# Fourteen seven-product pairs in each FFN, with sums by transfer, on a one-core transformer kernel

## What is computed

```
y    = x * rsqrt(mean(x*x) + EPS) * g           # per token
gate, up = split(y @ w_gu)                      # 1024 -> 2 * 2816
x    = x + 0.5 * ((silu(gate) * up) @ w_down)   # 2816 -> 1024
```

## Time and profile before

| | |
|---|---|
| median of 3 runs | 2190.74 us (2190.73 to 2190.77) |
| the profiled execution's own time | 2190.57 us |
| its span, first to last instruction | 2188.8 us |
| granted TensorE clock, mean | 1.000 |
| busy: PE, weight loads, DVE, ACT, POOL | 99%, 82%, 71%, 47%, 7% |

### The profile page before, as it was taken

The page is one execution under the profiler, slowest core; times in us unless marked ns, Lnnn a source line. Parts: engine busy times, 40 slices in busy tenths (PEclk is TensorE's granted clock), DMA queues, the critical chain, the costliest instruction groups (busy, mean ns, idle before and its releaser), DMA issues.

```text
span 2188.8 us, 30114 instructions
## 1 busy us (share of the span) xinstructions
PE 2173.2 (99%) x12152; PEld 1798.2 (82%) x12152; DVE 1564.9 (71%) x2421; ACT 1022.7 (47%) x1592; POOL 145.4 (7%) x112
## 2 busy tenths in 40 slices
PE   9999999999999999999999999999999999999999
PEld 7889897777778898988898887777788898977777
DVE  6768586988657685776777577777667685865873
ACT  5424244667544242334333245777544242438672
POOL 3000003000130000030000012000120000030000
PEclk9999999999999999999999999999999999999999
DMA  6333234131124334242423232222123333332211
GB/s 197 116 116 116 96 103 134 40 97 59 60 79 170 122 116 133 83 130 77 154 78 120 93 116 94 75 75 94 50 74 128 109 118 102 97 111 77 77 59 39
DMA packets 209714, 217.86 MB, mean 100 GB/s; under 512 B 3664, under 2 KB 205520, under 8 KB 209576
## 3 DMA queue, kind: packets, MB, share of 16 engines
q1 hardware_dynamic: 207184, 206.06, 29.1%
q0 software_dynamic: 1152, 5.44, 0.8%
q10 hardware_dynamic: 1240, 4.43, 0.5%
HBM read 213.79 MB, written 6.32 MB: 101 GB/s over the span
## 4 chain that ended last, share of the span: by engine, by line
PE 91%; DVE 4%; ACT 3%; issue 1%; DMA 0%; POOL 0%; SPq 0%; DVEq 0%; ACTq 0%
PE ps L1911 90%; PE ps L1915 1%; DVE sb_wlo L1278 1%; ACT sb_whi L730 1%; DVE sb_gla_ek L1617 0%; DVE sb_gla_eq L1620 0%; DMA sb_xT<-xT 0%; ACT sb_xh L730 0%; DVE sb_xT L1406 0%; ACT sb_hyb_th L730 0%; DVE sb_gla_xb L1612 0%; DVE sb_gla_cf L1609 0%; DVE sb_gla_d L1597 0%; DVE sb_xl L1300 0%; ACT sb_lnb L730 0%
## 5 line engine op out<-in xcount | busy, mean ns | idle before, releaser
L1911 PE MATMUL ps<-sb_xh,sb_whi 128*128 128x512 f32 (+1 forms) x1952 | 724.8, 371 | 1.8 <-DVE sb_xl L1700 0.8
L1911 PE MATMUL ps<-sb_xl,sb_whi 128*128 128x512 f32 (+1 forms) x1952 | 707.8, 364 | 0.1
L1911 PE MATMUL ps<-sb_xh,sb_wlo 128*128 128x512 f32 (+1 forms) x1952 | 705.7, 364 | 0.0
L730 ACT ACTIVATE sb_whi<-sb_raw 128x1024 fp32r<-128x1024 f32 (+1 forms) x368 | 377.7, 1033 | 360.5 <-PE ps L1911 353.0
L1278 DVE TENSOR_TENSOR sb_wlo<-sb_raw,sb_whi 128x1024 fp32r<-128x1024 f32 (+1 forms) x288 | 372.0, 1294 | 125.3 <-ACT sb_whi L730 123.7
L1911 PEld LDWEIGHTS ps<-sb_xh,sb_whi 128*128 128x128 f32 x1952 | 368.5, 189 | 76.7 <-issue 18.1
L1911 PEld LDWEIGHTS ps<-sb_xl,sb_whi 128*128 128x128 f32 x1952 | 368.8, 189 | 60.1 <-issue 3.1
L1911 PEld LDWEIGHTS ps<-sb_xh,sb_wlo 128*128 128x128 f32 x1952 | 368.4, 189 | 59.3
L1911 PE MATMUL ps<-sb_ffn_ah,sb_whi 128*128 128x512 f32 x704 | 275.3, 391 | 0.0
L1911 PE MATMUL ps<-sb_ffn_ah,sb_wlo 128*128 128x512 f32 x704 | 274.1, 389 | 0.0
L1911 PE MATMUL ps<-sb_ffn_al,sb_whi 128*128 128x512 f32 x704 | 273.9, 389 | 0.0
(11 more groups left out here) (288 smaller groups left out, 2593.3 us busy)
## 6 DMA issues: line engine op xcount, KB each, us to landing
sb_raw<-ffn_w_gu SPq DMA_DIRECT2D x86, 1024.0 KB, 5.2
sb_raw<-ffn_w_down SPq DMA_DIRECT2D x32, 1024.0 KB, 5.2
sb_raw<-w_ada SPq DMA_DIRECT2D x12, 1024.0 KB, 5.7
sb_raw<-ffn_w_down SPq DMA_DIRECT2D x16, 768.0 KB, 4.8
sb_raw<-gla_w_in SPq DMA_DIRECT2D x12, 1024.0 KB, 5.3
sb_raw<-diff_w_in SPq DMA_DIRECT2D x12, 1024.0 KB, 5.1
sb_raw<-w_in SPq DMA_DIRECT2D x10, 1024.0 KB, 5.2
sb_raw<-gla_w_out SPq DMA_DIRECT2D x4, 1024.0 KB, 5.1
```

The lines of the kernel that those rows point to most:

```text
L730: return e.activation(out, in_, func, bias=bias, scale=scale)
L1911: return e.matmul(out, lhsT, rhs, start=start, stop=stop, skip_group_check=skip)
```

## The change

Four edits are made together. FAST has fourteen pairs of each FFN instead of ten: 5, 10, 13 and 18 are added. The multiplication of up by the norm's factor goes away; the factor is multiplied onto each down sum instead, into a scratch tile (`gb`), and a second VectorE instruction adds that onto x. One of the four adds of `weight_sums` becomes a transfer issued by POOL, which adds a block of gate's weights onto up's in the raw panel (`gate_onto_up`). The low part of an activation is no longer VectorE's for all pairs but the last of a part: ACT writes minus the high part into `al`, and a transfer of POOL's queue adds the activation onto it. The sums of x are built in a buffer of their own (`ffn_xs`), which lies where four tiles of `al` are kept later. Half of the order on ACT and VectorE is rewritten to fit, and low parts of the activations have two more semaphores (`f_low0`, `f_low1`).

```diff
-FAST = ((6, 8, 9, 11, 12, 14, 16, 17, 19, 20),) * 4
+FAST = ((5, 6, 8, 9, 10, 11, 12, 13, 14, 16, 17, 18, 19, 20),) * 4
...
+            with ExitStack() as early:
+                x_sum[f] = sb(f"ffn{f}_xs", [128, 8, 256], F32, early)
+            al += tiles_of(sb(f"ffn{f}_al4", [128, 4, S], F32R, mem))
...
         def tail_late(j):
-            return j >= 5 and j not in (7, 15, 21)
+            return j >= 4 and j not in (7, 15, 21)
...
                         act(ah[:, j - k0, :], ub[j % 2][:, :], ACT.Copy).then_inc(sem["f_ah"], 1)
+                        if by_dma(J):
+                            act(al[j - k0], ub[j % 2][:, :], ACT.Copy, scale=-1.0).then_inc(sem["f_neg"], 1)
...
-                e.tensor_tensor(sums[:, 0:4, :], c_, d_, ALU.add).then_inc(sem["s_add"], 1)
-                w.wait_ge(sem["s_add"], 4 * i + 1)
-                e.tensor_tensor(c_, c_, a_, ALU.add).then_inc(sem["s_add"], 1)
-                e.tensor_tensor(sums[:, 4:8, :], sums[:, 0:4, :], a_, ALU.add).then_inc(sem["s_add"], 1)
-                w.wait_ge(sem["s_add"], 4 * i + 3)
+                w.wait_ge(sem[f"s_pre{i % 2}"], 16 * (i // 2 + 1))
+                e.tensor_tensor(sums[:, 4:8, :], c_, d_, ALU.add).then_inc(sem["s_add"], 1)
+                w.wait_ge(sem["s_add"], 3 * i + 1)
+                e.tensor_tensor(sums[:, 0:4, :], sums[:, 4:8, :], a_, ALU.subtract).then_inc(sem["s_add"], 1)
                 e.tensor_tensor(sums[:, 8:12, :], sums[:, 4:8, :], b_, ALU.add).then_inc(sem["s_add"], 1)
...
-                    def plain_up(j, u):
-                        used(w, u + 1)
-                        e.tensor_tensor(ub[j % 2][:, :], psum[f_banks[f]["pair", j][1]][:, :], rb[:, :],
-                                        ALU.mult).then_inc(sem["f_u"], 1)
...
+                    def up_free(j):
+                        if j >= 2 and by_dma(22 * f + j - 2):
+                            w.wait_ge(sem[low_done[22 * f + j - 2][0]], low_done[22 * f + j - 2][1])
...
-                            e.tensor_tensor(v, v, g, ALU.mult).then_inc(sem["f_p"], 1)
+                            up_free(j)
+                            used(w, u + 1)
+                            e.tensor_tensor(v, psum[f_banks[f]["pair", j][1]][:, :], g, ALU.mult).then_inc(sem["f_p"], 1)
...
-                        e.scalar_tensor_tensor(out=x[:, m, :], in0=psum[f_banks[f]["down", (part, m)][0]][:, :],
-                                               scalar=0.5, in1=x[:, m, :], op0=ALU.mult,
-                                               op1=ALU.add).then_inc(sem["f_x"], 1)
+                        e.scalar_tensor_tensor(out=gb[m % 2], in0=psum[f_banks[f]["down", (part, m)][0]][:, :],
+                                               scalar=0.5, in1=rb[:, :], op0=ALU.mult,
+                                               op1=ALU.mult).then_inc(sem["f_t"], 1)
+                        w.wait_ge(sem["f_t"], part_x(f, part, m))
+                        e.tensor_tensor(x[:, m, :], x[:, m, :], gb[m % 2], ALU.add).then_inc(sem["f_x"], 1)
...
-                w.wait_ge(sem["f_join"], 4 * i + 4)
-                e.tensor_tensor(up, up, rb[:, :], ALU.mult).then_inc(sem["f_u"], 1)
...
+            def gate_onto_up(f, j):
+
+                if j in FAST[f]:
+                    i = fast_before[f] + FAST[f].index(j)
+                    gate, up, off = fast_panels[i]
+                    for q in (gate, up):
+                        w.wait_ge(sem[f"raw{q % NRAW}"], 16 * (q // NRAW + 1))
+                    if i >= 2:
+                        w.wait_ge(sem["s_add"], 3 * i - 3)
+                    e.dma_start(raw[up % NRAW][:, 0:4, off:off + 128], raw[gate % NRAW][:, 0:4, off:off + 128],
+                                accum_op=ALU.add).then_inc(sem[f"s_pre{i % 2}"], 16)
+
+            def low_parts(f):
+
+                _, al, _, ub, _, _, _, _ = ffn_mem[f]
+                for k0, n in FF_PARTS[f]:
+                    for j in range(k0, k0 + 4):
+                        gate_onto_up(f, j)
+                    for j in range(k0, k0 + n):
+                        if j + 4 < k0 + n:
+                            gate_onto_up(f, j + 4)
+                        if by_dma(22 * f + j):
+                            w.wait_ge(sem["f_neg"], neg_made[22 * f + j])
+                            e.dma_start(al[j - k0].bitcast(F32), ub[j % 2][:, :],
+                                        accum_op=ALU.add).then_inc(sem[low_done[22 * f + j][0]], 16)
```

More of the change, by code:

```diff
@@ L581, in fast_source @@
             return raw[panel % NRAW][:, 0:nk, off:off + 128]
+        fast_panels = [(*W.fast[u][:2], W.units[u][1]) for u in W.fast if W.units[u][3] == "fa"]
         def lo_done(w, u):
@@ L674, in build, with by_dma @@
         f_banks = [ffn_banks(f) for f in range(4)]
+        low_done, n_vec, n_dma = {}, 0, [0, 0]
+        for f in range(4):
+            for k0, n in FF_PARTS[f]:
+                for j in range(k0, k0 + n):
+                    if FAST[f] and j < k0 + n - 1:
+                        n_dma[j % 2] += 1
+                        low_done[22 * f + j] = f"f_low{j % 2}", 16 * n_dma[j % 2]
+                    else:
+                        n_vec += 1
+                        low_done[22 * f + j] = "f_al", n_vec
+        def by_dma(J):
+            return low_done[J][0] != "f_al"
+        neg_made = rank([J for J in range(88) if by_dma(J)])
         def h_evac(w, k):
@@ L773, in ffn @@
             def ffn(f):
-                ah, _, gb, ub, _, sums, th, _ = ffn_mem[f]
+                ah, al, gb, ub, _, sums, th, _ = ffn_mem[f]
                 u = first[f"ffn{f}"]
@@ L821, in ffn @@
                         if j < 4:
-                            scaled_x(f, j, sums)
+                            scaled_x(f, j, x_sum[f])
                         silu(j)
@@ L833, in ffn @@
                             e.dma_start(bias_vec, bias_rows[:, :]).then_inc(sem["bias_dma"], 16)
[L834 to L840, removed]
                         if j < 4:
                             w.wait_ge(sem["t_vec"], 4 * (t_before[f] + j) + 3)
-                            act(th[:, j, :, :], sums[:, 8:16, :], ACT.Copy).then_inc(sem["t_act"], 1)
+                            act(th[:, j, :, :], x_sum[f][:, 4:8, :], ACT.Copy).then_inc(sem["t_act"], 1)
+                    if f == 2 and part == 0:
+                        w.wait_ge(sem["d_lam_mm"], 1)
+                        act(lam[:, 2:4], psum[FFN_AUX][:, 0:2], ACT.Exp).then_inc(sem["d_lam_e"], 1)
                     last = part == len(parts) - 1
@@ L1359, in ffn @@
                         if after_fast:
-                            scale_halves(f, j - 1, vgw[(j - 1) % 2], ub[(j - 1) % 2][:, :])
-                            product(j - 1)
+                            product(j - 1, None)
                         w_lo(u + 1)
@@ L1376, in ffn @@
                         u += 2
+                        if j < 4:
+                            x_sums(f, j, x_sum[f])
                         if not tail_late(j):
-                            plain_up(j, u - 2)
-                        if j < 4:
-                            x_sums(f, j, sums)
-                        if not tail_late(j):
-                            product(j)
+                            product(j, u - 2)
                         if j < 4:
                             w.wait_ge(sem["t_act"], t_act_before[f] + 3 * j + 3)
-                            e.tensor_tensor(tl[:, j, :, :], sums[:, 8:16, :],
+                            e.tensor_tensor(tl[:, j, :, :], x_sum[f][:, 4:8, :],
                                             th[:, j, :, :].bitcast(F32), ALU.subtract).then_inc(sem["t_vec"], 1)
@@ L1922, in rows @@
                     k = k0 + t
-                    w.wait_ge(sem[ready[0]], ready[1] + k + 1 + (h_y_ready[k] if ready[0] == "h_ylo" else 0))
+                    if ready[0] == "f_al":
+                        w.wait_ge(sem["f_ah"], ready[1] + k + 1)
+                        w.wait_ge(sem[low_done[ready[1] + k][0]], low_done[ready[1] + k][1])
+                    else:
+                        w.wait_ge(sem[ready[0]], ready[1] + k + 1 + (h_y_ready[k] if ready[0] == "h_ylo" else 0))
                     mm(psum[bank][:, :], hi[:, t, :], H[k], start and t == t0, False)
@@ L2013, in ffn @@
                             u += 1
-                        emptied[b] = "f_x", part_x(f, part, m)
+                        emptied[b] = "f_t", part_x(f, part, m)
                         if (part, m) in ADA_SUM:
@@ L2542, in pool_program @@
                 sum_squares(m)
+            low_parts(0)
             ffn_squares(0, KT)
```

79 lines of the change are left out of this document (39 added, 40 removed).

## The result

The changed kernel takes 2210.27 us (median of 4 runs, 2209.09 to 2211.32) against 2190.73 for the kernel before: ratio 1.0089, 95% interval 1.0073 to 1.0105. It is slower by 19.5 us. My 2192.0 and the range up to 2202 were both too low. The profiled execution after has a span of 2209.4 us, 20.6 more than before.

The account below looks back on a forecast made before the run. TensorE, busy 99% of the span, was taken to bound the kernel. 2190.57 - 12.8 for matmuls + 14.1 for new waits gave 2191.9, set at 2192.0 us against the median; range 2178 to 2202.

Parts of the forecast that it names:

- Matmuls: TensorE, all FFNs: 16 more fast pairs save 0.80 us each, 12.8 us in all.
- VectorE in runs: Consecutive fast pairs 8 to 14: VectorE needs 9.4 us per pair, below TensorE's 10.08, so no wait.
- The tail: Last-part down sums: 0.72 us more per step, making waits of 3.7, 4.7, 5.0 and 0.7 us at FFN ends.
- the last term: End of FFN 3 to the last block: one addition, 0.72 less 0.1, a wait of 0.7 us.
- The clock: TensorE after the new waits at FFN ends: forecast with no fall to 1.2 GHz, so no cost.
- rival A: New FFN-end waits drop TensorE's clock, 2.5 us a fall, three give 2199.5; chance 0.27.
- Transfers: POOL's queue in fast pairs: 256 KB transfers take 3.7 us and cost nothing; they cost only above 6.7 each.
- Rival C: Late transfers hold the third join of fast pairs; from 6.7 us each they delay TensorE, 2204 at 7.0; chance 0.15.
- Rival B: FFN ends: the added waits are hidden in full or by two thirds, giving 2177.9 to 2187; chance 0.20.
- the 14.1 us: Sum of the forecast new TensorE waits at the ends of the four FFNs.
- The likeliest case: Whole kernel: the forecast with the ends of its per-pair and tail-step terms, 2189.5 to 2194.5 us.

Follow-up runs that it names:

- e8: e3 with pair 5 plain again in FFN 1 alone: 2178.15 us.
- e10: e9 with the low parts of all activations made by VectorE again, without their transfers and second ScalarE copies: 2177.99 us.
- e12: e10 with the fourth weight sum on VectorE too, leaving POOL's queue no transfer in the FFNs: 2187.10 us.
- e5: The kernel before, with each down sum in the last part of each FFN made by two VectorE instructions: 2213.88 us.
- e3: The changed kernel with the norm's factor multiplied onto up again in each FFN's last part, one VectorE instruction per down sum there: 2188.98 us.
- e6: e3 with the ten fast pairs of before: 2190.43 us.
- e2: The changed kernel with pair 5 plain again in FFN 1 alone: 2197.43 us.
- e7: e3 with the 4 MB bias broadcast issued at the second down sum of part 0 of FFN 1: 2179.15 us.
- e11: e3 with the low parts of activations on VectorE, the broadcast staying at pair 5 of FFN 1: 2179.71 us.
- e1: The changed kernel with the 4 MB bias broadcast issued at pair 9 of FFN 1 instead of pair 5: 2208.32 us.
- e9: e3 with the 4 MB bias broadcast issued at pair 2 of FFN 2: 2183.35 us.

## Why the prediction was wrong

**Matmuls: right.** 10.08 us per fast pair, and e8 with 15 more of them than before stands 2190.55 - 2178.15 = 12.4 us below it, where 15 x 0.80 is 12.0; e10 with 16 stands 12.6 below.

**VectorE in runs: right, and with room.** 9.4 us per pair left no gap in runs of seven; e10 shows that even steps of 10.6 in a run of five leave none. e12 shows where the room ends.

**The tail: right.** 0.72 per step was 0.71; the waits forecast as 3.7, 4.7, 5.0 and 0.7 were 3.4, 4.2, 4.25 and 0.6 (by its own rows the last term is 0.72 less 0.16, so 0.6). At the end of FFN 2 the place was off: TensorE stopped for the low part of tile 7, ahead of POOL's sum. e5 shows that the second instruction by itself makes the waits at the ends of FFN 0 to 2, and e3 that they go with it.

**The clock: the step that failed first.** The forecast took 2192.0 with no fall, and left the falls to rival A at 0.27. All three came, and a fourth. The rival's price of 2.5 us a fall was near: 2.6, 2.3, 3.4 and 3.2 us are read at the four places. My ground for leaving it out was that "no row shows a fall after a wait", but before no wait was longer than 1.5 us, so the trace could not show one. The Trainium skill, "TensorE: Matmul & The Clock Gate", section "What's actually happening", has the rule that an idle engine goes back to the half rate, and the four windows above agree. With three falls the sum was 2199.5, still inside the range; the fourth wait, which I had not forecast, carried the time beyond it.

**Transfers: the step that failed second.** "I take 3.7: nothing" was near for the landing: the medians after are 4.2 and 4.3 us.

```profile
sb_raw<-ffn_w_down SPq DMA_DIRECT2D x32, 1024.0 KB, 6.6
sb_ffn_al<-sb_ffn_u POOLq DMA_DIRECT2D x76, 256.0 KB, 4.3
sb_raw<-sb_raw POOLq DMA_DIRECT2D x56, 256.0 KB, 4.2
```

In the steady runs this cost nothing (e6, e8). The trace before had a bound for it that I did not use: I wrote that no transfer of this queue beside VectorE is in it, but `sb_dif_bias` is, eight transfers of 448 KB that landed in 3.2 to 4.1 us in the second mixer, with VectorE busy about three quarters of the time. What failed is that I priced the transfers in the steady run only, and left the panels behind the broadcast out of the sum altogether. What I missed was at the end of part 0 of FFN 1: a fast pair keeps both its panels until its last unit, so with pair 5 fast SyncE asks for the down panels 16.6 us later; they now stand behind 4 MB of broadcast, which itself comes 6.2 us earlier than before; and between the activation and the first down sum there is now a transfer of 6.7 us where an instruction of 0.7 was. Together 9.3 us and a fall. e2, e7 and e11 each take away one of the three and most of the wait. The sign stood in the trace before: the three panels asked for behind the broadcast there took 18 to 21 us as well. Rival C had the right kind of cause at the wrong place, and its threshold of 6.7 us per transfer plays no part: in e6 single transfers took up to 11.2 us, and it cost nothing.

Put together: 2192.0, less 1.6 for the waits that were shorter, 9.2 for the three falls at the ends and 11.6 at the fourth place give 2211.2; the profiled execution took 2211.16, the median is 2210.27.

Rival B did not come, and its range was wrong as well: with two thirds of the 14.1 us gone, 4.7 are left and the time is 2182.6, not 2187. The likeliest case, by the ends that it names for its terms, spans 2189.8 to 2193.8 and not 2189.5 to 2194.5. Neither changes what came out.

One thing is open: which gaps make the clock fall, and for how long. After the four waits of the changed kernel it fell, after the 2.0 us of e11 it did not, and after the 1.9 us of e2 it did.

## What to carry to other kernels

A scaling moved from before a matmul to after it can take work off a busy stretch and put it onto the one chain that the next stage waits for; do it for all parts but the last. e8 and e10 keep the whole gain that way and stand at 2178.15 and 2177.99 us against 2190.6. Count a new wait of a few microseconds on TensorE at once and a half, what it waits and what the clock takes after it: here 32.8 us for 21.3 us of waits. Before a producer is replaced by a transfer, look at who stands behind it in the queue and at the largest other transfer of the program, at the end of each stage and not only in its middle.

## What was not expected of the hardware

A 4 MB transfer from and to device memory slows panels of 1 MB for some 20 us: one issued 3 us after it landed after 21 us, where the median is 6.6, and three behind it in the kernel before took 18 to 21.5, where the median is 5.2. What that costs depends on who waits. Nothing came of it before, in e8 and in e10. In the other kernels TensorE's wait was 9.3 or 8.7 us at the place of the change, 2.0 of them without the activation's transfer behind the panel (e11), 7.7 in e1, 1.3 in e7, and 4.0 in e9, which went with the transfers queued on POOL (e10).

And 0.7 us more for each of 32 down sums costs 23 us (e5): its two groups of waits are 14.3 us in all, so about a third of the cost lies in what TensorE does after them.
